# Two hybrid joints of a four-layer fp32 kernel: first rows transposed before the last closing half piece, weight parts and residuals in another order

## The reference, cut to what matters

```python
def rmsnorm(x, w):
    y = x * lax.rsqrt(jnp.mean(x * x, axis=-1, keepdims=True) + EPS)
    return y * w

def hybrid_layer(x, c_act, ...):
    shift, scale, gate = jnp.split(c_act @ w_ada + b_ada, 3, axis=-1)
    h = rmsnorm(x, norm_w) * (1.0 + scale) + shift
    proj = h @ w_in                 # 1024 columns of h against 11264 columns of w_in
    ...
    return x + gate * (merged @ w_out)
```

## Time and profile before

| | |
|---|---|
| median of 3 runs | 1052.53 us (1051.22 to 1054.04) |
| span of the profiled execution | 1051.6 us |
| time of the profiled execution beside its span | not listed apart; the span is 0.9 us under the median |
| TensorE busy | 1011.8 us (96%) |
| VectorE busy | 702.0 us (67%) |
| ScalarE busy | 555.5 us (53%) |
| GpSimd busy | 198.4 us (19%) |
| DMA | 192.15 MB, mean 183 GB/s |
| chain that ended last | PE 88%, DVE 8%, ACT 2% |

### The profile page before, as it was taken

How to read it: one execution, slowest core, us unless ns; L and a number is a source line. 1 busy time by engine, 2 the same in 40 slices (tenths; PEclk the granted TensorE clock), 3 DMA queues, 4 the chain that set the end, 5 groups by cost and what they waited for, 6 DMA issues and landing times.

```text
span 1051.6 us, 15169 instructions
## 1 busy us (share of the span) xinstructions
PE 1011.8 (96%) x6020; PEld 889.0 (85%) x6020; DVE 702.0 (67%) x1104; ACT 555.5 (53%) x847; POOL 198.4 (19%) x206
## 2 busy tenths in 40 slices
PE   6899999999999899999999999989999999999996
PEld 5678889877978689998899888868999889988884
DVE  7984846877758656667766586665445555757666
ACT  6668577566346554445443344545444555334543
POOL 5800160000000006423213100000665000420000
PEclk9999999999999999999999999999999999999998
DMA  7543434767736289875656446546776446645551
GB/s 264 179 125 107 139 113 138 258 210 230 214 127 218 92 290 315 295 252 184 200 171 192 141 141 199 182 138 180 236 236 220 121 132 185 184 141 153 186 181 40
DMA packets 95351, 192.15 MB, mean 183 GB/s; under 512 B 8577, under 2 KB 11905, under 8 KB 95281
## 3 DMA queue, kind: packets, MB, share of 16 engines
q1 hardware_dynamic: 91440, 179.53, 54.7%
q0 software_dynamic: 3408, 11.18, 3.0%
q10 hardware_dynamic: 432, 0.49, 0.1%
HBM read 189.59 MB, written 1.05 MB: 181 GB/s over the span
## 4 chain that ended last, share of the span: by engine, by line
PE 88%; DVE 8%; ACT 2%; issue 1%; DMA 0%; ACTq 0%; DVEq 0%
PE G L631 15%; PE G L633 14%; PE G L632 14%; PE G L640 8%; PE G L643 8%; PE G L642 8%; DVE WL L1596 2%; PE G L673 2%; PE G L675 2%; PE G L674 2%; PE B L594 2%; PE B L945 1%; PE B L767 1%; PE B L788 1%; PE B L977 1%
## 5 line engine op out<-in xcount | busy, mean ns | idle before, releaser
L1596 DVE TENSOR_TENSOR WL<-RAW,WH 128x1024 fp32r<-128x1024 f32 (+2 forms) x294 | 369.8, 1260 | 245.0 <-ACT WH L1085 244.2
L1085 ACT ACTIVATE WH<-RAW 128x1024 fp32r<-128x1024 f32 (+2 forms) x294 | 308.1, 1050 | 279.6 <-PE G L633 139.3
L631 PE MATMUL G<-WH,HTh 128*128 128x512 f32 (+2 forms) x556 | 225.1, 405 | 9.3 <-DVE WL L1596 9.2
L640 PE MATMUL G<-HTh,WH 128*128 128x256 f32 x768 | 219.4, 286 | 0.4 <-DVE HTl L1695 0.3
L643 PE MATMUL G<-HTh,WL 128*128 128x256 f32 x768 | 217.3, 283 | 0.0
L642 PE MATMUL G<-HTl,WH 128*128 128x256 f32 x768 | 217.3, 283 | 0.0
L633 PE MATMUL G<-WL,HTh 128*128 128x512 f32 (+2 forms) x556 | 215.4, 387 | 0.0
L632 PE MATMUL G<-WH,HTl 128*128 128x512 f32 (+2 forms) x556 | 214.7, 386 | 0.0
L640 PEld LDWEIGHTS G<-HTh,WH 128*128 128x128 f32 x768 | 147.0, 191 | 2.3 <-issue 1.8
L642 PEld LDWEIGHTS G<-HTl,WH 128*128 128x128 f32 x768 | 147.1, 191 | 0.7 <-issue 0.5
L643 PEld LDWEIGHTS G<-HTh,WL 128*128 128x128 f32 x768 | 146.9, 191 | 0.0
(11 more groups left out here) (369 smaller groups left out, 1351.6 us busy)
## 6 DMA issues: line engine op xcount, KB each, us to landing
RAW<-in_w_in SPq DMA_DIRECT2D x176, 512.0 KB, 4.0
RAW<-in_even_w_in SPq DMA_DIRECT2D x40, 512.0 KB, 3.7
AR<-in_w_ada_t SPq DMA_DIRECT2D x32, 512.0 KB, 4.9
RAW<-in_odd_w_in SPq DMA_DIRECT2D x16, 512.0 KB, 4.2
AR<-in_w_ada_g POOLq DMA_DIRECT2D x32, 256.0 KB, 4.2
RAW<-in_w_proj_ret SPq DMA_DIRECT2D x16, 512.0 KB, 3.8
RAW<-in_w_out SPq DMA_DIRECT2D x16, 512.0 KB, 3.7
RAW<-in_even_w_out SPq DMA_DIRECT2D x12, 512.0 KB, 4.4
```

Of the source, the lines that this page charges most:

```text
L631: nc.tensor.matmul(o, xh, wh, start=begins, stop=False)
L640: nc.tensor.matmul(o, fh, h_[:, kx, :], start=begins and f % 2 == 0, stop=False, skip_group_check=True)
L1085: return nc.scalar.activation(out_, ps, ACT.Copy, **kw)
L1596: vt(wl, raw, wh.bitcast(F32), ALU.subtract).then_inc(*dve.mark(LO, n))
```

## The change

TensorE gets `hybrid_turn(l, ti)` in the place of `norm_turn` at the two hybrid joints. It takes four PSUM banks instead of two, and puts the even and the odd column blocks of each half q in a bank of their own. For ti = 0 it is issued ahead of the last closing half (`time == 2 * H0[0] - 1`, `time == 215`) instead of behind it; for ti = 1 it is issued ahead of the last opening half of ti = 0 (behind i = 2) instead of behind it. The affine step is split by block for every r: ScalarE does the even block, VectorE the odd one (for ti = 0, r = 0 VectorE does both). ScalarE makes `hi(n0+1)` and `hi(n0+2)` ahead of the squares and `hi(n0+3)` behind the squares of ti = 0. VectorE makes `lo(n0+1)` and `lo(n0+2)` each behind a residual of ti = 0, ahead of `rstd(l, 0)`; `residual(l-1, 1, 1)` stands behind `turned(l, 0, 1)`, and `turned(l, 0, 3)` behind `scaled(l, 1)`. The joints 0 to 1 and the end of the kernel keep their order. The number of transposes, matmuls and weight parts is the same.

```diff
@@ -433,7 +433,7 @@
...
             made[2 * c0 - 5], made[2 * c0 - 3] = [c0, c0 + 1], [c0 + 2, c0 + 3]
-            made[2 * c0 - 1], made[2 * c0 + 1] = [c0 + 4], [c0 + 5]
+            made[2 * c0 - 1], made[2 * c0 + 1] = [c0 + 4], []
             for i in range(1, 6):
@@ -470,8 +470,8 @@
...
         HT_HI, HT_LO = events("ht_hi", TURNS), events("ht_lo", TURNS)
-        HN_B, HN_D = (events(f"hn_{e}", [(l, ti, r) for l in (2, 3) for ti in L2 for r in rs])
-                      for e, rs in (("b", (0, 1)), ("d", (2, 3))))
+        HN_B = events("hn_b", [(l, ti, r) for l in (2, 3) for ti in L2 for r in H4 if ti or r])
+        HN_D = events("hn_d", [(l, ti, r) for l in (2, 3) for ti in L2 for r in H4])
         RES_V = events("res_v", [(l, ti, n) for l in L2 for ti in L2 for n in L2]
@@ -728,30 +728,37 @@
...
 
-                ps = take(("nt", l, ti, q), (HT_LO if l < 2 else HN_D if q else HN_B).of(l, ti, 2 * q + 1))
+                ps = take(("nt", l, ti, q), HT_LO.of(l, ti, 2 * q + 1))
                 pe.wait_ge(l_ci, 16)
...
                 else:
-                    pe.wait_ge(*((HN_A if l else HN_P) if q else HN_V).of(l, ti))
+                    pe.wait_ge(*(HN_P if q else HN_V).of(l, ti))
                 for j in range(4):
...
 
+            def hybrid_turn(l, ti):
+
+                for q in range(2):
+                    pe.wait_ge(*(HN_A if q else HN_V).of(l, ti))
+                    for j in range(2):
+                        ps = take(("nt", l, ti, q, j), HT_HI.of(l, ti, 2 * q + 1))
+                        for i in range(2):
+                            c = 512 * q + 256 * i + 128 * j
+                            ins = nc.tensor.transpose(ps[:, 128 * i:128 * i + 128], HN[:, ti, c:c + 128], IDENT)
+                        ins.then_inc(*told("nt", l, ti, q, j))
+
             def open_layer(l, first):
 
-                if l not in UNSCALED:
-                    for q in range(2):
-                        norm_turn(l, 0, q)
                 for i in range(2 * OPEN[l]):
...
                         norm_turn(l, 1, 1)
-                    if l not in UNSCALED and i == 3:
-                        for q in range(2):
-                            norm_turn(l, 1, q)
+                    if l not in UNSCALED and i == 2:
+                        hybrid_turn(l, 1)
 
@@ -1035,6 +1042,8 @@
...
             for time in range(2 * groups["zr"]["at"] + 2 * OPEN[1], 2 * H0[0]):
+                if time == 2 * H0[0] - 1:
+                    hybrid_turn(2, 0)
                 half(time)
@@ -1053,6 +1062,8 @@
...
                 for time in range(2 * OPEN[2 + l], 216):
+                    if l == 0 and time == 215:
+                        hybrid_turn(3, 0)
                     half(2 * H0[l] + time)
@@ -1111,28 +1122,30 @@
...
 
-                ps = bank_of["nt", l, ti, r // 2]
                 rows = slice(128 * ti, 128 * ti + 128)
-                if l > 1 and r > 1:
-                    act.wait_ge(*HN_D.of(l, ti, r))
-                else:
+                if l < 2:
+                    ps = bank_of["nt", l, ti, r // 2]
                     act.wait_ge(*side("nt", l, ti, r // 2))
...
                         j = k % 4
-                        if l < 2:
-                            ins = copy(HTh[:, k, rows], ps[:, 128 * j:128 * j + 128],
-                                       scale=co[("even_g", "odd_g")[l]][:, k:k + 1])
-                        else:
-                            act.wait_ge(*MOD.of(l - 2, "c"))
-                            ins = nc.scalar.activation(HN32[:, k, rows], ps[:, 128 * j:128 * j + 128], ACT.Identity,
-                                                       scale=Acols[l - 2][:, k:k + 1], bias=Bcols[l - 2][:, k:k + 1])
-                    if l > 1:
-                        ins.then_inc(*act.mark(HN_B, l, ti, r))
-                        act.wait_ge(*HN_B.of(l, ti, r))
-                if l > 1:
-                    c = slice(2 * r, 2 * r + 2)
-                    ins = copy(HTh[:, c, rows], HN32[:, c, rows])
-                ins.then_inc(*act.mark(HT_HI, l, ti, r))
+                        ins = copy(HTh[:, k, rows], ps[:, 128 * j:128 * j + 128],
+                                   scale=co[("even_g", "odd_g")[l]][:, k:k + 1])
+                    ins.then_inc(*act.mark(HT_HI, l, ti, r))
+                    return
+                c = slice(2 * r, 2 * r + 2)
+                act.wait_ge(*HN_D.of(l, ti, r))
+                if ti or r:
+                    act.wait_ge(*HN_B.of(l, ti, r))
+                copy(HTh[:, c, rows], HN32[:, c, rows]).then_inc(*act.mark(HT_HI, l, ti, r))
+
+            def affine(l, ti, r):
+
+                k, c = 2 * r, 128 * (r % 2)
+                act.wait_ge(*side("nt", l, ti, r // 2, 0))
+                act.wait_ge(*MOD.of(l - 2, "c"))
+                nc.scalar.activation(HN32[:, k, 128 * ti:128 * ti + 128],
+                                     bank_of["nt", l, ti, r // 2, 0][:, c:c + 128], ACT.Identity, scale=Acols[l - 2][:, k:k + 1],
+                                     bias=Bcols[l - 2][:, k:k + 1]).then_inc(*act.mark(HN_B, l, ti, r))
 
@@ -1149,6 +1162,9 @@
...
                 n0 = (0, 54, H0[0], H0[1])[l]
+                if l not in UNSCALED:
+                    hi(n0 + 1)
+                    hi(n0 + 2)
                 square(l - 1, 0, 0)
@@ -1165,20 +1181,23 @@
...
                 square(l - 1, 0, 1)
-                hi(n0 + 2)
+                hi(n0 + 3)
                 scaled(l, 0)
+                if l == 2:
+                    square(l - 1, 1, 0)
                 turned(l, 0, 0)
-                if l < 3:
-                    square(l - 1, 1, 0)
-                turned(l, 0, 1)
-                turned(l, 0, 2)
-                turned(l, 0, 3)
                 if l == 3:
                     square(l - 1, 1, 0)
+                affine(l, 0, 1)
+                turned(l, 0, 1)
+                affine(l, 0, 2)
+                turned(l, 0, 2)
                 square(l - 1, 1, 1)
-                hi(n0 + 3)
+                affine(l, 0, 3)
+                turned(l, 0, 3)
                 scaled(l, 1)
                 for r in range(4):
+                    affine(l, 1, r)
                     turned(l, 1, r)
@@ -1676,11 +1695,11 @@
...
 
-                dve.wait_ge(*side("nt", l, ti, r // 2))
+                dve.wait_ge(*side("nt", l, ti, r // 2, 1))
                 dve.wait_ge(*MOD.of(l - 2, "c"))
-                for k in (2 * r, 2 * r + 1):
-                    c = 128 * (k % 4)
-                    ins = ts(HN32[:, k, 128 * ti:128 * ti + 128], bank_of["nt", l, ti, 1][:, c:c + 128],
+                c = 128 * (r % 2)
+                for k in (2 * r + 1,) if ti or r else (0, 1):
+                    ins = ts(HN32[:, k, 128 * ti:128 * ti + 128], bank_of["nt", l, ti, r // 2, k % 2][:, c:c + 128],
                              Acols[l - 2][:, k:k + 1], Bcols[l - 2][:, k:k + 1], ALU.mult, ALU.add)
@@ -1703,6 +1722,8 @@
...
                 residual(l - 1, 0, 0)
+                if l not in UNSCALED:
+                    lo(n0 + 1)
                 residual(l - 1, 0, 1)
@@ -1719,26 +1740,24 @@
...
                     return
+                lo(n0 + 2)
                 rstd(l, 0)
...
                 residual(l - 1, 1, 0)
-                residual(l - 1, 1, 1)
+                for r in range(3):
+                    affine(l, 0, r)
                 turned(l, 0, 0)
-                affine(l, 0, 2)
                 affine(l, 0, 3)
                 turned(l, 0, 1)
-                lo(n0 + 2)
+                residual(l - 1, 1, 1)
                 turned(l, 0, 2)
-                turned(l, 0, 3)
                 rstd(l, 1)
                 scaled(l, 1)
+                turned(l, 0, 3)
                 lo(n0 + 3)
-                turned(l, 1, 0)
-                affine(l, 1, 2)
-                turned(l, 1, 1)
-                affine(l, 1, 3)
-                turned(l, 1, 2)
-                turned(l, 1, 3)
+                for r in range(4):
+                    affine(l, 1, r)
+                    turned(l, 1, r)
                 lo(n0 + 4)
```

## The result

The changed kernel takes 1042.72 us (median of 4, 1041.90 to 1043.69), the kernel before beside it 1052.79 us. The ratio is 0.9904, 95% interval 0.9875 to 0.9932: faster by 10.1 us in the medians, about 1%, with the interval wholly under 1. The forecast was 1042.9, in a range of 1039.5 to 1047.5.

What follows compares the result with a forecast made beforehand. TensorE was taken to bound the kernel, with 14.2 us of idle time or slow clock at the two hybrid joints. Gains of 6.1 + 3.5 = 9.6 us, nothing for the clock, made 1052.5 - 9.6 = 1042.9 us, range 1039.5 to 1047.5.

Steps and rivals of the forecast that it cites:

- (a): First joint, VectorE: `lo(n0+1)` changes place with the first residual; the second residual ends as before.
- (b): First joint, VectorE: `lo(n0+2)` ahead of `rstd`, partly in 0.69 us idle time, costs about 0.45 us.
- Steps (c) to (e): First joint: early transposes end at 345.5, first opening half at 346.95 instead of 347.98, then idles of 0.3 and 0.45 us.
- Step (f): First joint, ti = 1: each r takes 1.27 us across VectorE and ScalarE, under a half's 1.40; halves end at 359.95.
- Rival 2: VectorE to ScalarE hand-over at each r is slower, say 1.8 us: 5.8 us lost in all, 1048.7 us; chance 0.08.
- The sum: Gains of 6.1 us at the first joint and 3.5 at the second, 9.6 us in all.
- Rival 3: Stage behind the joints gives the won time back if its weights come no earlier: 1050 to 1053 us; chance 0.08.
- Rival 4: Slower: a late load of n0+2 stops the whole joint; at 8.9 us in both joints 1048.2 us; chance 0.04.
- Rival 5: Early turn fails as rows come late: about 1.0 us less at each joint, 1045 us; chance within the forecast's 0.57.
- Rival 1: Clock falls all the same in one or both hybrid joints: 1044.5 us for one, 1046.0 for both; chance 0.23.
- the 0.9 us between median and span: Median of the kernel before stands 0.9 us above its profiled span of 1051.6 us, so the forecast starts from 1052.5.

Runs made afterwards that it cites:

- the filled kernel: Kernel before with sixteen extra transposes (another run: eight matmuls) in TensorE's idle stretch at both hybrid joints: 1051.22 us (matmuls 1050.83).
- the late high part: Changed kernel with the high part of n0+2 written four times over, as if its load came 3.3 us later: 1046.75 us.
- the last experiment: Changed kernel with residual (2, 1, 1) moved ahead of turned(3, 0, 1), plus the w_ada_t products one half piece later: 1040.91 us.
- the two fills: Kernel before with extra work in TensorE's idle stretch at both hybrid joints: eight matmuls 1050.83 us, sixteen transposes 1051.22 us.
- the weight parts put back: Changed kernel with the weight parts in the order of the kernel before: 1045.18 us.
- two more moves: Changed kernel, second joint only: low part of n0+2 ahead of residual (2, 0, 1), residual (2, 1, 1) ahead of turned(3, 0, 1): 1043.16 us.

## Why the prediction was right

| us from the end of the second-last closing half | first joint, forecast | measured | second, forecast | measured |
|---|---|---|---|---|
| transposes of ti = 0 start | 0.35 | 0.27 | 1.0 | 1.00 |
| first opening half | 2.86 | 2.81 | 3.5 | 3.54 |
| transposes of ti = 1 | 7.36 | 7.25 | 9.6 | 9.50 |
| half with n0+3 | 8.86 | 8.72 | 11.1 | 10.97 |
| end of the joint | 15.86 | 15.78 | 18.1 | 18.05 |

**Steps (a) and (b).** VectorE after, first joint:

```profile
340.13 0.15 DVE L1665 TENSOR_SCALAR SM<-SM 128x1 f32<-128x1 f32 x1
340.31 0.22 DVE L1668 TENSOR_SCALAR SM<-SM 128x1 f32<-128x1 f32 x1
...
342.10 0.49 DVE L1693 TENSOR_SCALAR TK<-X,SM 128x512 f32<-128x512 f32 x1
...
351.84 0.42 DVE L1718 TENSOR_TENSOR HTl<-AR,HTh 128x256 fp32r<-128x256 f32 x1 [0.49 <-ACT HTh L1096]
352.19 0.41 DVE L1702 TENSOR_SCALAR AR<-B,SM 128x128 f32<-128x128 f32 x1
353.08 0.43 DVE L1718 TENSOR_TENSOR HTl<-AR,HTh 128x256 fp32r<-128x256 f32 x1 [0.48 <-ACT HTh L1096]
```

The 0.69 us idle ahead of the second `rstd` instruction is gone, and `scaled` starts 1.79 us behind it, as before. The cost of `lo(n0+2)` there, forecast 0.45 us, is 0.38: before, the scaling started 0.65 us ahead of the end of the second-last closing half (343.44 against 344.09), now 0.27 (342.10 against 342.37). **Steps (c) to (e)** are the table. **Step (f)**, one r in 1.27 us, is 1.24 (351.84 to 353.08), under a half of 1.40, and the four halves of ti = 1 run without a gap. Rival 2 falls by that. One price was wrong without harm: GpSimd's first add at the second joint, taken as 1.27 us, took 2.21, and VectorE's `scaled` still started 0.46 us behind the end of the second-last closing half, where 0.47 was forecast. `lo(n0+4)` was ready 0.4 us before it was wanted.

**The sum**, 6.1 + 3.5, was 6.18 + 3.56. **Rival 3** falls by the stage between the joints, 316.39 us. **Rival 4** is a real path, and no load was late enough. Its price has a slip: a load of 8.9 us in both joints comes 4.8 later than 4.1, which over slacks of 1.4 and 2.3 costs 3.4 + 2.5 us, so 1048.8 and not 1048.2. **Rival 5** is priced too high at the second joint: with the transposes behind the closing half it is 0.15 us longer, not 1.0. **Rival 1**, the low clock at the joints, did not come: not in the profile after and not in seven others with the transposes of ti = 1 in the new place, sixteen joints in all. The one time it came in a variant of the changed kernel was with these transposes put back. I took nothing for it because the stretches hold transposes, and the filled kernel bears that out. But the waits had also become short, at most 1.06 us in the profile after, and at these joints no wait of 1.74 us or less was followed by a low clock, with or without transposes. Which of the two kept the clock up in the changed kernel is not separated.

Where the working was loose: the 0.9 us between median and span. The profiled execution of before was one of the slower ones, with three low stretches; 1.8 us stand around a span, so its own time was about 1053.4 (an estimate, 1051.6 + 1.8), and the profile after has 11.5 us less span, not 9.6. That the median still came out at 0.2 from the forecast is because the medians differ by about what the joints do. A hit that close is luck: single executions of the changed kernel lie between 1041.90 and 1043.69 us.

## What to carry to other kernels

When one engine writes the order of another's idle time, replay the new order by hand on the durations of the trace, engine by engine: here all ten points of the table came out within 0.15 us of the chip. Put work that needs nothing new (transposes for the next half, the last product of the old stage) exactly where the bounding engine would wait; here that shortened the waits, and no joint with it had a low clock. And look at what stands behind a waiting instruction in its queue: moving one residual ahead of a blocked step gave another 1.1 us, while moving a weight part to where its load had only just landed and GpSimd was still adding took back 0.8.

## What had not been expected

- At the hybrid joints, TensorE's waits of 2.12 to 2.54 us were followed by the 1.2 GHz level five times (four times in the two profiles of the kernel before, once with the second rows turned late), and once, after 2.16 us with the late high part, they were not. The low level lasted about 3.4 us four times and about 7 us once. The same 2.0 us wait at the joint 0 to 1 was followed by clock 0.50 in five profiles and by 1.00 in the eight others without a fill. Four of these eight had a low stretch near 62 us instead. A low stretch ahead of the first joint goes with a step of about 1.6 us between executions of the same kernel.
- A late w_ada_t load cost TensorE 1.1 to 2.5 us in four of the fourteen profiles, through two queues; VectorE stood in front of that load for 2.8 us or more in every profile but that of the last experiment.
- GpSimd's first add into X at the second joint took 2.21 us in all nine profiles in which a `lo` had started 0.2 us ahead of it, and 1.3 us in the five others (the kernel before twice, the two fills, the weight parts put back). The `lo` took 1.22 us all the same. With two more moves a `lo` started 0.97 us ahead of the end of that add, and took 2.04 us. So in both cases the one that started second was longer by about what the first still had to run (0.9 against 1.1, 0.8 against 1.0 us). The cause was not tried.
